# Half of a context network's hidden features back from plain fp32 to split products, and a later first gathered dot, in a two-block transformer kernel

## The reference, cut to what matters

```
def swiglu(h, w_gate, w_up, w_down):
    return (jax.nn.silu(h @ w_gate) * (h @ w_up)) @ w_down
...
            xc = xc + g1c * yc
            hc = rms_norm(xc, norm_ffn[i]) * (1.0 + sc2c) + sh2c
            xc = xc + g2c * swiglu(hc, w_gate[i], w_up[i], w_down[i])
```

## Time and profile before

| | us |
|---|---|
| median of 3 runs | 3975.88 |
| lowest and highest of them | 3972.86, 3977.01 |
| the profiled execution's own time | 3978.74 |
| its span in the profile | 3976.9 |

### The profile page before, as it was taken

The page is one execution under the profiler, slowest core; times in us unless marked ns, Lnnn a source line. Parts: engine busy times, 40 slices in busy tenths (PEclk is TensorE's granted clock), DMA queues, the critical chain, the costliest instruction groups (busy, mean ns, idle before and its releaser), DMA issues.

```text
span 3976.9 us, 55816 instructions
## 1 busy us (share of the span) xinstructions
PE 3823.1 (96%) x22529; PEld 3304.4 (83%) x22529; DVE 2328.4 (59%) x4053; ACT 1570.5 (39%) x2531; POOL 693.6 (17%) x586
## 2 busy tenths in 40 slices
PE   8999999989999989999999999998899999889998
PEld 5788776778899889999999999786677777667887
DVE  6455333546888467777777776557633345664333
ACT  4523342444345543333333333536522233564222
POOL 0112000244112343222233221201100010101000
PEclk9999999999999999999999999998999999999999
DMA  5211235533355678888888886312234342203332
GB/s 207 81 41 44 102 118 200 177 99 99 108 176 198 212 238 294 289 277 284 274 283 283 285 285 196 113 55 62 82 118 136 122 143 69 74 26 87 99 97 75
DMA packets 209184, 617.19 MB, mean 155 GB/s; under 512 B 18464, under 2 KB 68640, under 8 KB 205088
## 3 DMA queue, kind: packets, MB, share of 16 engines
q1 hardware_dynamic: 168352, 465.76, 36.6%
q0 software_dynamic: 40576, 147.87, 10.8%
HBM read 583.67 MB, written 29.88 MB: 154 GB/s over the span
## 4 chain that ended last, share of the span: by engine, by line
PE 85%; DVE 7%; ACT 4%; DMA 2%; issue 2%; POOL 0%; SPq 0%; DVEq 0%; ACTq 0%; POOLq 0%
PE ps L598 22%; PE ps L609 21%; PE ps L600 21%; PE ps L555 6%; PE ps L3443 2%; PE ps L2513 1%; DMA raw<-w_in 1%; PE ps L2540 1%; PE ps L887 1%; DVE hlo_plain L764 1%; ACT whi L522 1%; PE ps L2121 1%; PE ps L2531 1%; PE ps L1218 1%; PE ps L1209 1%
## 5 line engine op out<-in xcount | busy, mean ns | idle before, releaser
L598 PE MATMUL ps<-hhi,whi 128*128 128x512 f32 (+1 forms) x2824 | 1075.9, 381 | 6.8 <-DVE xres L3049 2.9
L600 PE MATMUL ps<-hlo,whi 128*128 128x512 f32 (+1 forms) x2824 | 1048.8, 371 | 0.1
L530 DVE TENSOR_TENSOR wlo<-raw,whi 128x1024 fp32r<-128x1024 f32 x543 | 671.3, 1237 | 635.6 <-ACT whi L522 628.2
L522 ACT ACTIVATE whi<-raw 128x1024 fp32r<-128x1024 f32 x594 | 625.7, 1054 | 601.7 <-PE ps L609 452.8
L609 PE MATMUL ps<-hhi,wlo 128*128 128x512 f32 (+1 forms) x2824 | 670.3, 376 | 9.0 <-DVE wlo L530 9.0
L598 PEld LDWEIGHTS ps<-hhi,whi 128*128 128x128 f32 x2824 | 532.9, 189 | 108.6 <-issue 25.4
L600 PEld LDWEIGHTS ps<-hlo,whi 128*128 128x128 f32 x2824 | 533.3, 189 | 68.8 <-issue 4.1
L609 PEld LDWEIGHTS ps<-hhi,wlo 128*128 128x128 f32 x2824 | 513.2, 189 | 83.7 <-DVE wlo L530 9.4
L600 PE MATMUL ps<-ag_lo,whi 128*128 128x384 f32 x1024 | 342.0, 334 | 0.0
L598 PE MATMUL ps<-ag_hi,whi 128*128 128x384 f32 x1024 | 342.0, 334 | 0.0
L3646 POOL DMA_INDIRECT fetched<-peer_v_rows,rows x128 | 151.3, 1182 | 359.9 <-DVE xtok L3618 335.7
(11 more groups left out here) (652 smaller groups left out, 6018.7 us busy)
## 6 DMA issues: line engine op xcount, KB each, us to landing
raw<-w_in SPq DMA_DIRECT2D x151, 512.0 KB
raw<-peer_u SPq DMA_DIRECT2D x128, 512.0 KB
raw<-peer_v SPq DMA_DIRECT2D x128, 512.0 KB
raw<-w_mod SPq DMA_DIRECT2D x96, 512.0 KB
raw<-w_gate SPq DMA_DIRECT2D x66, 512.0 KB
raw<-w_up SPq DMA_DIRECT2D x66, 512.0 KB
raw<-w_down SPq DMA_DIRECT2D x66, 512.0 KB
gate_dram<-stage SPq DMA_DIRECT2D x24, 1024.0 KB, 4.3
```

The source lines that it names most:

```text
L522: a.x.activation(whi[n % NW][:], raw[i % NRAW][:], ACT.Copy, bias=0.0, scale=1.0).then_inc(*a.gives("hi", i))
L530: e.x.tensor_tensor(wlo[n % NW][:], raw[i % NRAW][:], whi[n % NW][:].bitcast(F32), ALU.subtract).then_inc(*e.gives(*lo_sig(i)))
L598: t.x.matmul(o, w, p.hi, start=grp.opens and k == 0, stop=False)
L600: t.x.matmul(o, w, p.lo, start=False, stop=False)
```

## The change

Three things are edited.

1. `cnet` is direct in its first half alone (22 gate and up units, 11 down units). The 33 units of the second half are split: `whi` on ScalarE, `wlo` on GpSimd (the ring's `lo` argument was ("vector", "gpsimd") already, but had no use while all was direct). Their input is split too: eight more activations on ScalarE make `hchi`, eight subtractions on GpSimd make `c0apart`, a new buffer of eight blocks. The inner features of the second half are split as well: 11 activations (`f10h`, ScalarE) and 11 subtractions (VectorE). VectorE no longer waits for the down units before it overwrites `f10w`.
2. The stream `experts` has one more empty step at its head on each engine, and `expert_tensor` begins with `yield Every(14.0)`: the first dot is placed later.
3. Since the planner's costs of a split unit and its splits differ from those of a direct one, it places the side streams otherwise from the second half of `cnet` on, on every engine.

The diff, cut to its core:

```
         def scalar(self, a):
...
-                if self.only:
+                if self.apart:
                     a.x.activation(p.plain, p.plain, ACT.Identity, bias=self.shift(c), scale=1.0).then_inc(
                         *a.gives("apply_a", self.name, "moved", c))
                     continue
...
+            for c, p in enumerate(self.pairs if self.apart else []):
+                a.wait_ge("apply_a", self.name, "moved", c)
+                a.x.activation(p.hi, p.plain, ACT.Copy, bias=0.0, scale=1.0).then_inc(*a.gives("apply_a", self.name, "hi", c))
...
         def gpsimd(self, g):
-            if self.once:
-                for c in range(0 if self.only else 3):
+            if self.apart:
+                g.wait_ge("apply_v", self.name, "made", KC - 1)
+                g.wait_ge("route_t", "scores", 15)
+                for c, p in enumerate(self.pairs):
+                    g.wait_ge("apply_a", self.name, "hi", c)
+                    g.x.tensor_tensor(p.lo, p.plain, p.hi.bitcast(F32), ALU.subtract).then_inc(
+                        *g.gives("apply_g", self.name, "lo", c))
+            elif self.once:
+                for c in range(3):
...
     class Network:
...
-                        u.direct = "up" in direct
+                        u.direct = self.direct and half == 0
...
-                    u.direct = "down" in direct
+                    u.direct = self.direct and half == 0
...
+        def undivided(self, k):
+
+            return self.direct and k < HALF
...
     def fup_vector(v, i, phase):
...
-            if f.whole and k >= HALF:
-                v.wait_ge(*last_of("fdown", (f, 0, (7 * HALF + k - HALF) // 8)))
...
-        elif not f.whole:
+        elif not f.undivided(k):
...
     def expert_tensor(t):
+        yield Every(14.0)
         for i in range(257):
             yield Every(3.96)
...
     def expert_vector(v):
+        yield
         v.wait_ge("tap_v", 7)
...
         for i in range(NF - 1):
             fetch(i)
+        yield
         for i in range(128):
```

More of the change, by code:

```diff
@@ L770, in vector @@
                         yield
-            for c in [] if self.only else range(3, KC) if self.once else [KC - 1]:
+            for c in [] if self.apart else range(3, KC) if self.once else [KC - 1]:
                 self.lower_vector(v, c)
         def gpsimd(self, g):
-            if self.once:
-                for c in range(0 if self.only else 3):
+            if self.apart:
[7 more added lines that the diff above has]
+                for c in range(3):
                     p = self.pairs[c]
@@ L3092, in __init__ @@
                             groups.append(Group([], (self, half, o), k == 0, False))
-                        if self.whole:
-                            groups[-1].pairs.append(Pair(None, None, ("ffn_v", nm, "up", HALF * half + k), None, self.whole[k]))
+                        if self.direct and half == 0:
+                            groups[-1].pairs.append(Pair(None, None, ("ffn_v", nm, "up", k), None, self.plain[k]))
                         else:
@@ L3107, in fgate_scalar @@
         if k >= 2:
-            a.wait_ge("ffn_v", f.name, "up" if f.whole else "lo", k - 2)
+            a.wait_ge("ffn_v", f.name, "up" if f.undivided(k - 2) else "lo", k - 2)
         for s in f.free:
@@ L3115, in product @@
     def product(f, k):
-        return f.whole[k % HALF] if f.whole else held(("out", "fup", (f, k)))[:, 0:f.n] if f.v else f.sg[k % 2]
+        return f.plain[k] if f.undivided(k) else held(("out", "fup", (f, k)))[:, 0:f.n] if f.v else f.sg[k % 2]
     def fup_vector(v, i, phase):
@@ L3134, in fup_scalar @@
         f, k = spine[i].key
-        if phase and not f.whole:
+        if phase and not f.undivided(k):
             a.wait_ge("ffn_v", f.name, "up", k)
@@ L3630, in expert_scalar @@
     def expert_scalar(a):
-        for i in range(128):
+        for i in range(129):
             yield
@@ L3694, in program @@
     c0out = mixer_pairs(cm0)
+    c0apart = [sb(f"c0apart{c}", kb, [TC], F32R)[:] for c, kb in enumerate((121, 122, 123, 124, 134, 135, 205, 206))]
     cffn = Apply("c0ffn", cnorm, "c0ffn", HC, lambda c: amod[:, 0, 1, 1, c:c + 1], lambda c: modv(0, 1, 24 + c), once=True,
-                 plain=True, late=[mod_ready(0)], before=("apply_v", "c0mix", "made", KC - 1))
-    cnet = Network(0, 1, TC, cffn.pairs, list(range(145, 152)) + list(range(168, 185)), "clate", ("vector", "gpsimd"), [], ("up", "down"))
+                 apart=c0apart, late=[mod_ready(0)], before=("apply_v", "c0mix", "made", KC - 1))
+    cnet = Network(0, 1, TC, cffn.pairs, list(range(145, 152)) + list(range(168, 185)), "clate", ("vector", "gpsimd"), [], cffn.whole)
     c1mix = Apply("c1mix", cnorm, "c1mix", HC, lambda c: amod[:, 1, 1, 0, c:c + 1], lambda c: modv(1, 1, c), once=True,
```

21 lines of the change are left out of this document (11 added, 10 removed).

## The result

The changed kernel takes 3971.78 us (median of 20 runs, 3966.9 to 3976.35), the kernel before 3977.22 us beside it (20 runs, 3972.86 to 3985.28). The ratio is 0.9987, its 95% interval 0.9981 to 0.9993: a gain of about 5 us where 13 had been forecast.

What follows compares the result with a forecast made beforehand. It took TensorE, busy 3823 of 3977 us, to bound the kernel. Its terms, -19.0 + 3.1 + 2.5 - 3.0 + 7.0 - 5.0 + 1.0, gave -13.4 us and a forecast of 3963 us, range 3950 to 3987.

Steps and rivals of the forecast that it cites:

- its own signs: Trace signs of error: idle TensorE inside split units, a lower clock in the 25 steps, or a 9 us `gin` wait.
- 33 units split again: Second half of the context network: split units take 2.88 us against 3.46 direct, 0.58 less each, -19.0 us.
- 27 switches in the network: Dense steps between split matmuls cost 0.08 us extra each; with 12 more in `cm1`, 39 in all, +3.1 us.
- waits in the network: Split part: sixteen VectorE products of two SBUF inputs are held up by GpSimd's low parts, +2.5 us (0 to +19).
- `cm1`, 12 switches among it: 15 dense steps moved into `cm1` fill TensorE's recurrence waits, -3.0 us (-5 to +3); its 12 switches cost 0.08 each.
- 25 steps alone: Dense steps behind `cm1` run at VectorE's pace, 1.17 us against TensorE's 0.89, +7.0 us (0 to 22).
- first `peer_u` units: The 10.4 us stall goes, but a 5.4 us one for the first `gin` comes: -5.0 us (-9.6 to -1.5).
- end of `experts`: The last sum stands behind the last `peer_u` unit's low part, +1.0 us (0 to 3).
- later dot doesn't help, gin as late: Rival, first `peer_u` units: `gin` is as late as the fetched row, the stall stays 10.4 us, 3967.5; chance 0.12.
- GpSimd's order: Rival, network: TensorE waits for odd dense steps' scaling queued behind GpSimd's low parts, +9.3 us, 3985; chance 0.10.
- half clock: Rival: the 25 steps behind `cm1` run at half clock, +15.0 us more, 3977.5; chance 0.10.
- rival on the read port: Rival, split part: all 16 VectorE products blocked 2.0 us by GpSimd low parts, 32 us, 3981.5; chance 0.10.

Runs made afterwards that it cites:

- pace4: Changed kernel with the planner allowed to place the next dense step while the fullest other engine leads TensorE by up to 4 us; 3960.01 us.
- lo_vector: Changed kernel with the low parts of the context network's second half on VectorE in place of GpSimd; 3970.86 us.
- pace2: Changed kernel with the planner allowed to place the next dense step while the fullest other engine leads TensorE by up to 2 us; 3966.28 us.
- pace4_lodown: pace4 with the low parts of the network's last 11 units, the down units, on VectorE in place of GpSimd; 3959.17 us.
- gin_alone: Changed kernel with `gin` 1 loaded behind the fifth `peer_u` unit and the first five fetches held until `gin` 0 has landed; 3967.14 us.
- split_alone: Changed kernel with the dots back at their old place, leaving only the split of the network's second half; 3972.89 us.
- dot_alone: Kernel before with only the later order of the dots, nothing split again; 3965.92 us.

## Why the prediction was right, and where its sum was off

The direction was right and the range held the time; the likeliest time, 3963, was 9 us too low. That the range held says little: it is 37 us wide, and all eleven other kernels above, from 3959 to 3973 us, lie in it too. By the stretch: forecast -13.4, measured -2.8 (the medians have -5.4, with an interval of the ratio from -2.8 to -7.6). By its own signs the text was in part wrong: TensorE has idle time amid the split units, ahead of pieces of the apply, and the wait for `gin` is 8.24 us and not 1 to 6.

| term | forecast | measured | from |
|---|---|---|---|
| 33 units split again | -19.0 | -19.0 | units 2.88 us apart again |
| 27 switches in the network | +2.1 | 0.0 | a step there takes its own 0.89 |
| slower clock in the first pair, not in the sum | | +1.3 | 9.99 - 8.67 |
| waits in the network | +2.5 | +4.7 | its four waits |
| rest of the network, not in the sum | | +1.4 | 270.12 - 317.32 + 19.0 + 40 x 0.89 - 4.72 - 1.3 |
| `cm1`, 12 switches among it | -3.0 + 1.0 | 0.0 | 70.17 - 56.85 - 15 x 0.89 |
| 25 steps alone | +7.0 | +8.0 | 30.26 - 25 x 0.89 |
| first `peer_u` units | -5.0 | } +0.8 | 1077.53 - 1076.71 |
| end of `experts` | +1.0 | } | |

**Units.** Right to the digit. The network is 47.2 us shorter; the text said some 55 before waits and switches.

**Switches.** The term was counted twice. From the start of the step's first matmul to the next fp32r matmul are 0.81 us, and that one takes 0.20 to the next start (1288.43, 1289.24, 1289.44): together 1.01, which is the step's 0.89 and the 0.12 of a split matmul. The 0.08 by which 0.20 exceeds 0.12 is a part of the 0.89 that the earlier trace rows gave for a step. 24 steps stand in this way among the split matmuls of the network without a wait beside them, and 23 of them come to 0.89 within 0.01 us. The "rest" of 1.4 us I haven't followed: the matmuls that start anew behind a wait and the small pieces of the apply are in it.

**Waits in the network.** The mechanism was named and is there: sixteen products took 13.9 us more (16 had been the estimate), and three waits for VectorE came of it, 2.64 us (2.5). The fourth, 2.08 us for a high part, I had not seen: ScalarE stood behind a high part of the hidden features, whose product waited on VectorE behind three instructions of the routing of 2.3 us each (L3392 among them only beside a low part of GpSimd; it takes 0.28 us in pace4), and a table load came on top:

```profile
1220.63 0.39 ACT L3152 ACTIVATE f10h<-ps 128x256 fp32r<-128x256 f32 x1 [5.33 <-DVE ps L3140]
```

"It was at 53%" said nothing about that, since ScalarE's queue is in order. The Trainium skill (SBUF — State Buffer, Who interferes with whom) says that VectorE with two SBUF inputs and GpSimd reading SBUF exclude each other; the products of 1.51 and 1.86 us in the mean, and lo_vector's 0.67 to 0.75 with GpSimd idle, agree.

**`cm1`.** The step that failed is "what they can do is fill such waits". They filled next to none: the wait for the recurrence is 4.52 us for 3.37, its neighbour 1.31 for 1.54, and TensorE's idle time in the stage 6.25 us for 5.71; about 1 us came back by the clock (0.95 for 0.92). What was late is VectorE's part of the recurrence:

```profile
1363.63 4.12 DVE L2329 SCALAR_TENSOR_TENSOR c_Sen<-c_Sen,c_dec 128x128 f32<-128x128 f32 x6
1367.68 1.22 DVE L3471 TENSOR_TENSOR onehot<-ps,iT 128x1024 f32<-128x1024 f32 x1
...
1364.31 2.39 POOL L530 TENSOR_TENSOR wlo<-raw,whi 128x1024 fp32r<-128x1024 f32 x1 [1.12 <-ACT whi L522]
...
1370.88 1.28 ACT L2220 ACT_TABLE_LOAD   x1 [6.74 <-DVE c_gvT L2286]
```

L2329 has eight instructions ahead of the wait, most of 0.35 us. One of them took 2.56 us beside the low part shown and one 1.58 beside the low part before it, and a one-hot stands behind them; in the kernel before, one took 2.43 and no one-hot stood there. ScalarE is not what is full: it stood idle for 6.74 us, until VectorE was through. The number of dense steps doesn't explain it either: in pace4, with 2 of them in `cm1`, two of these instructions took 2.49 and 2.47 us and the wait is 7.02; in pace2, with 17, only one was longer, 0.89, and the wait is 3.05. So low parts of GpSimd that fall on the recurrence are a part of the wait. They are not the whole of it: pace4_lodown has one of 2.37 us, like the kernel before, and a wait of 5.25. No run here moves the low parts of `cm1`, so this is read from rows and not tried.

**25 steps.** VectorE was read right as the pace (1.13 a step in place of 1.17), and the clock stayed at 1.00; 1.21 in the mean, by waits of 0.96, 0.87 and 1.29 us for a copy.

**First `peer_u` units.** This is the term that was most wrong, and two of its inputs were. "The first gin" as what is late next was right, so, nearly, was its issue (D + 5.4 forecast, D + 5.9 by the row). But its landing was sized at 9.5 us by one fetch, and it took 13.5: it lies behind five fetches on the wire, which gin_alone shows to cost 5 us. And the slow clock behind a wait of 8.24 us cost 2.4 us and not 1.4 (from the unit's first matmul to its low part's 5.25 us, 2.88 in the same kernel's first unit). Together the whole 10.4 us that the stall had cost was given back, which is why the later dot was worth nothing (split_alone). The rival "later dot doesn't help, gin as late", chance 0.12, had this mechanism; its 3967.5 kept the other terms of the forecast. So the branch that the forecast gave one chance in two is not the one that happened.

**End of `experts`.** dot_alone's 10.1 us less against a stall of 10.4 leaves 0.3 for it; 1.0 was forecast.

Added up: -19.0 + 0.0 + 1.3 + 4.7 + 1.4 + 0.0 + 8.0 + 0.8 = -2.8. The rivals "GpSimd's order" and "half clock" did not happen: no wait of TensorE in the network ends with a scaling or low part of GpSimd, and the 25 steps ran at 1.00. The rival on the read port happened in part: the sixteen products took 13.9 us more, not 32, but short instructions, which it left out, were held up as well.

## What to carry to other kernels

A direct piece that is made cheaper on TensorE takes its cover along: the work that stood beside it must be placed again, and here that, not the split, decided between -2.8 and -14.6 us. Before moving a load behind other work, write down what else is issued in the 10 us ahead of it on every queue; a load behind five gathers takes the gathers' time too. And a part that pays by itself can be worth nothing in company, so run each alone: the dot alone gave 10 us, the split alone 3, both together 3.

## What the runs showed of the hardware that was not expected

**A short VectorE instruction can pay for a whole low part of GpSimd.** In pace4, while GpSimd made low parts, three `TENSOR_SCALAR` of 128x128 took 4.06 us and a `SCALAR_TENSOR_TENSOR` 2.38 (rows above); in the changed kernel one took 2.43, and the recurrence in `cm1` has such ones in every kernel (the longest between 0.89 and 2.56 us in place of 0.35):

```profile
1207.08 2.40 POOL L530 TENSOR_TENSOR wlo<-raw,whi 128x1024 fp32r<-128x1024 f32 x1 [1.18 <-ACT whi L522]
1207.14 2.43 DVE L3369 TENSOR_SCALAR rank<-rank 128x128 f32<-128x128 f32 x1
...
L3369 DVE TENSOR_SCALAR rank<-rank x3: 227/227/2427, 1101.2 to 1207.1; 128x128 f32<-128x128 f32 x3
```

Its median is 0.227 us; begun 0.06 us into a low part it ended 0.09 us after that. It has one SBUF input only. The Trainium skill (same page and section) says that `tensor_scalar` can enter a mode in which it takes the shared pair of ports, and that whoever comes second waits for the whole of the first; the row agrees. What a meeting costs does not depend on the size of the blocked instruction, so counting only the sixteen large products was too narrow. The one-hots, which read PSUM and SBUF, kept their 1.21 us everywhere.

**Transfers.** `gin` of 1536 KB took 7.7 us with a slab of weights beside it, 12.9 with five fetches ahead, and 13.5 with a second `gin` behind it as well. In pace2 it took 15.5 (1422.40 to its first use at 1437.87), with a second `gin` and three of the five fetches issued behind it; the context's result had landed at 1419.84, ahead of it, so what made it longer there is open.
